# An address change: split operands move from residue 64 and 128 to residue 192 modulo 256 bytes

## What is computed

```python
# first layer
h = rms_norm(x, norm1_w);  proj = h @ w_in                # 2048 x 5648
x = x + concat([attn(q, k, v), ssm(z, xbc, dt)]) @ w_out  # 2048 x 2048
h = rms_norm(x, norm2_w);  u = causal_dwconv(h @ w_up)    # 2048 x 11264
x = x + (silu(u_gate) * u_val) @ w_down                   # 5632 x 2048
# second layer
h = rms_norm_2(x, g) * (1 + scale) + shift
proj = h @ w_in_2                                         # 2048 x 7168
x = x + gate * (concat([y_a, y_r]) @ w_out_2)             # 2048 x 2048
out = rms_norm_2(x, final_gain)
```

## Time and profile before

| what | value |
|---|---|
| median of 3 runs | 1540.4 us (1539.52 to 1541.3) |
| span of the profiled execution | 1537.5 us |
| TensorE busy (matmuls) | 1524.5 us, 12,586 instructions |
| TensorE busy (weight loads) | 1483.7 us |
| VectorE busy | 1136.1 us |
| ScalarE busy | 778.1 us |
| read from memory | 335.97 MB, 220 GB/s over the span |
| granted TensorE clock | full in all 40 slices |

### The profile page before, as it was taken

The page is one execution under the profiler, slowest core; times in us unless marked ns, Lnnn a source line. Parts: engine busy times, 40 slices in busy tenths (PEclk is TensorE's granted clock), DMA queues, the critical chain, the costliest instruction groups (busy, mean ns, idle before and its releaser), DMA issues. The chain is left out here.

```text
span 1537.5 us, 32072 instructions
## 1 busy us (share of the span) xinstructions
PE 1524.5 (99%) x12586; PEld 1483.7 (97%) x12586; DVE 1136.1 (74%) x1373; ACT 778.1 (51%) x930; POOL 29.8 (2%) x56
## 2 busy tenths in 40 slices
PE   9999999999999999999999999999999999999997
PEld 8999997999999999999999999999999989999997
DVE  7877777657987878788788887879854644764754
ACT  7645455545554444444444444445554643454554
POOL 0000000000000000000000000000000000000000
PEclk9999999999999999999999999999999999999999
DMA  9474556457877767677686776866465554445451
GB/s 348 171 272 161 200 177 220 146 171 273 302 282 249 288 233 273 244 249 274 235 293 229 262 272 221 300 219 217 150 247 194 196 193 162 160 159 185 154 186 58
DMA packets 85932, 339.23 MB, mean 221 GB/s; under 512 B 9680, under 2 KB 10208, under 8 KB 79328
## 3 DMA queue, kind: packets, MB, share of 16 engines
q1 hardware_dynamic: 77760, 281.05, 52.1%
q0 software_dynamic: 7232, 54.55, 10.1%
q10 hardware_dynamic: 864, 2.53, 0.4%
HBM read 335.97 MB, written 2.12 MB: 220 GB/s over the span
## 5 line engine op out<-in xcount | busy, mean ns | idle before, releaser
L683 DVE TENSOR_TENSOR wlo<-raw,whi 128x1024 fp32r<-128x1024 f32 x528 | 643.3, 1223 | 345.9 <-ACT whi L320 342.2
L320 ACT ACTIVATE whi<-raw 128x1024 fp32r<-128x1024 f32 x528 | 557.5, 1059 | 646.5 <-PE PS L1328 573.6
L1324 PE MATMUL PS<-gh,whi 128*128 128x256 f32 x3096 | 863.7, 279 | 0.7 <-DVE gl L1208 0.3
L1326 PE MATMUL PS<-gl,whi 128*128 128x256 f32 x3096 | 856.1, 277 | 0.0
L1328 PE MATMUL PS<-gh,wlo 128*128 128x256 f32 x3096 | 856.1, 277 | 0.0
L1324 PEld LDWEIGHTS PS<-gh,whi 128*128 128x128 f32 x3096 | 581.7, 188 | 5.9 <-issue 2.6
L1326 PEld LDWEIGHTS PS<-gl,whi 128*128 128x128 f32 x3096 | 581.4, 188 | 0.8
L1328 PEld LDWEIGHTS PS<-gh,wlo 128*128 128x128 f32 x3096 | 581.6, 188 | 0.0
L1324 PE MATMUL PS<-ah,whi 128*128 128x256 f32 x688 | 189.9, 276 | 0.0
L1328 PE MATMUL PS<-ah,wlo 128*128 128x256 f32 x688 | 189.9, 276 | 0.0
L1326 PE MATMUL PS<-al,whi 128*128 128x256 f32 x688 | 189.9, 276 | 0.0
(11 more groups left out here) (256 smaller groups left out, 894.6 us busy)
## 6 DMA issues: line engine op xcount, KB each, us to landing
raw<-weights SPq DMA_DIRECT2D x528, 512.0 KB, 3.6
ada_w<-w_ada POOLq DMA_DIRECT2D x48, 1024.0 KB, 5.9
EM<-rows POOLq DMA_DIRECT2D x1, 3072.0 KB, 12.4
X<-xT SPq DMA_DIRECT2D x3, 512.0 KB, 8.3
c<-const ACTq DMA_DIRECT2D x1, 1536.0 KB, 7.1
c_act<-c_rows POOLq DMA_DIRECT2D x1, 1024.0 KB, 7.0
outT<-X SPq DMA_DIRECT2D x2, 512.0 KB, 3.2
outT<-X SPq DMA_DIRECT2D x3, 256.0 KB, 2.2
```

The lines of the kernel that those rows point to most:

```text
L320: act.activation(whi[:, j % SPLIT, :], raw[:, j, :], ACT.Copy).then_inc(s_hi, 1)
L683: dve.tensor_tensor(wlo[:, j % SPLIT, :], raw[:, j, :], whi[:, j % SPLIT, :].bitcast(F32), ALU.subtract).then_inc(s_lo, 1)
L1324: pe.matmul(out[:, t, :], whi[:, b, w], hi[:, kt, :], start=first and half == 0 and (apart or t % 2 == 0), stop=False, skip_group_check=True)
L1326: pe.matmul(out[:, t, :], whi[:, b, w], lo[:, kt, :], start=False, stop=False, skip_group_check=True)
```

## The change

It moves addresses; no instruction is added, dropped or moved on any engine.

- The four slots of whi and of wlo are 1,088 numbers long instead of 1,024. 4,352 bytes are 17 times 256, so each slot still begins at residue 128.
- A new function `shifted` gives 16 for the units of the blocks in NAT and NAT2, and 0 for the others. Where it gives 16, ScalarE and VectorE write a unit 16 numbers (64 bytes) further into its slot, and `product_nat` reads it there: its moving operand begins at residue 192 instead of 128.
- The gaps around gh and gl and ahead of ah and ah2 are chosen anew: gh, gl, ah, al, ah2 and al2 begin at residue 192 instead of 64. That is the moving operand of `product` and the stationary one of `product_nat`. The stationary operand of `product` stays at 128.
- Buffers behind gl stand 1,792 bytes further (7 times 256), and SQX2 2,048 bytes; their residues stay.

```diff
--- before.py
+++ after.py
@@ -54,10 +54,18 @@
 
 
 NAT, NAT2 = (9, 10), (6, 7, 10, 13)
+NAT_SHIFT = 16
 CONVERTED = (80, 81, 82, 83, 87, 91)
 OUT_TILES = [8, 9, 10, 11, 12, 13, 14, 15, 0, 1, 2, 3, 4, 5, 6, 7]
 OUT_UNITS = ([(0, k) for k in range(5)] + [(1, k) for k in range(5)] + [(0, 5), (1, 5)] + [(0, 6), (0, 7), (1, 6), (1, 7)]
              + [(2, k) for k in range(8)] + [(3, k) for k in range(8)])
+
+
+def shifted(blk):
+
+    if not isinstance(blk, int):
+        return 0
+    return NAT_SHIFT if blk - B_IN in NAT or blk - B_IN2 in NAT2 else 0
 
 
 def head_tile(low, high, h):
@@ -103,13 +111,12 @@
 
         X, _ = place("X", [P, DT, S])
         raw, _ = place("raw", [P, RAW, 1024])
-        whi, _ = place("whi", [P, SPLIT, 1024], F32R)
-        wlo, _ = place("wlo", [P, SPLIT, 1024], F32R)
-        at[0] += 192
+        whi, _ = place("whi", [P, SPLIT, 1024 + 64], F32R)
+        wlo, _ = place("wlo", [P, SPLIT, 1024 + 64], F32R)
+        at[0] += 64
         gh, _ = place("gh", [P, DT, S], F32R)
-        at[0] += 0
         gl, _ = place("gl", [P, DT, S], F32R)
-        at[0] += 192
+        at[0] += 64
         prm, _ = place("prm", [P, N_PARAMS])
         cst, _ = place("cst", [P, 3 * P + 32])
         rb, _ = place("rb", [P, S])
@@ -150,10 +157,10 @@
         UV, o = place("UV", [P, 4, S + 2], offset=o)
         CG, o = place("CG", [P, 4, S], offset=o)
         CV, o = place("CV", [P, 4, S], offset=o)
-        ah, o = place("ah", [P, 4, S], F32R, offset=o)
+        ah, o = place("ah", [P, 4, S], F32R, offset=o + 128)
         al, o = place("al", [P, 4, S], F32R, offset=o)
-        SQX2, o = place("SQX2", [P, 2, 4, S], offset=o)
-        ah2, o = place("ah2", [P, 4, S], F32R, offset=o)
+        SQX2, o = place("SQX2", [P, 2, 4, S], offset=o + 128)
+        ah2, o = place("ah2", [P, 4, S], F32R, offset=o + 128)
         al2, o = place("al2", [P, 4, S], F32R, offset=o)
 
         TH, _ = place("TH", [P, 8, S], offset=area)
@@ -317,7 +324,8 @@
                 blk, j = blk + j // RAW, j % RAW
                 act.wait_ge(s_raw[j], blk * 16 + 16)
                 act.wait_ge(s_used, blk * RAW + j + 1)
-                act.activation(whi[:, j % SPLIT, :], raw[:, j, :], ACT.Copy).then_inc(s_hi, 1)
+                first = shifted(blk)
+                act.activation(whi[:, j % SPLIT, first:first + 1024], raw[:, j, :], ACT.Copy).then_inc(s_hi, 1)
 
             def group(blk):
                 for j in range(8):
@@ -680,8 +688,9 @@
 
                 blk, j = blk + j // RAW, j % RAW
                 dve.wait_ge(s_hi, blk * RAW + j + 1)
-                dve.tensor_tensor(wlo[:, j % SPLIT, :], raw[:, j, :], whi[:, j % SPLIT, :].bitcast(F32),
-                                  ALU.subtract).then_inc(s_lo, 1)
+                first = shifted(blk)
+                dve.tensor_tensor(wlo[:, j % SPLIT, first:first + 1024], raw[:, j, :],
+                                  whi[:, j % SPLIT, first:first + 1024].bitcast(F32), ALU.subtract).then_inc(s_lo, 1)
 
             def group(blk):
                 for j in range(8):
@@ -1364,7 +1373,7 @@
             def product_nat(b, par, tiles, first, last):
 
                 for half in range(2):
-                    kt, w = tiles[half], slice(512 * half, 512 * half + 512)
+                    kt, w = tiles[half], slice(NAT_SHIFT + 512 * half, NAT_SHIFT + 512 * half + 512)
                     for c in range(2):
                         out, m = PS[:, 2 * par + c, :], slice(P * c, P * c + P)
                         pe.matmul(out, gh[:, kt, m], whi[:, b, w], start=first and half == 0, stop=False,
```

## The result

| | median us | range us | runs |
|---|---|---|---|
| before | 1540.39 | 1539.48 to 1541.3 | 5 |
| after | 1581.84 | 1581.17 to 1582.72 | 5 |

The ratio is 1.027 (95% interval 1.0259 to 1.0281): the kernel is slower, by 41.5 us. The time is inside the range (1514 to 1588), but on the other side than forecast.

What follows compares the result with a forecast made beforehand. The prediction took TensorE's pace through its matmuls to bound the kernel. Its terms, 0 - 3.9 - 1.3 = -5.2 us, took 1540.4 us to 1535 us, with a range of 1514 to 1588.

Steps and rivals of the forecast that it cites:

- What bounds the kernel: Whole kernel: TensorE's pace through its stream of matmuls sets the end; other engines have room for a stream some per cent faster.
- Part 1: ScalarE and VectorE writing 64 bytes further for six blocks, with longer slots: cost 0, either way.
- Part 2: 10,657 fast `product` matmuls, moving residue 64 to 192: pace stays 113.3 ns, cost 0; bounds -15 and +48 us.
- Part 3: 863 `product` matmuls at the slow pace of 117.8 ns fall into the fast pace: -3.9 us.
- The 112 ns of the bare weight load: Loads of 128 stationary columns by themselves, read as 112 ns each; `product` at 113.3 ns stands 1.3 ns above.
- Part 4: 576 `product_nat` matmuls, moving residue 128 to 192, stationary 64 to 192: pitch 228.9 to 226.7 ns, -1.3 us.
- Rival C: `product` stream falls into the slow pace and stays: +48 us for everything, 1588 us; loop alone 1567; chance 0.25.
- Rival E: Distance between the two operands' residues counts: 2.2 ns more on each of 11,520 `product` matmuls, +25 us, 1566 us; chance 0.10.
- Rival B: Pace of `product` itself falls, since 192 is a better start for the moving stream: 1520 us; chance 0.17.
- The rule of the Trainium skill: TensorE has two read ports of its own, one per operand, and never waits; by it the change gives no difference.

## Why the prediction was wrong

- **What bounds the kernel**: right. TensorE's pitch times its matmuls gives the change to 2 us; the other engines only wait longer.
- **Part 1**, the shifted writes and the longer slots cost nothing: right, 1059 and 1224 ns, and the kernel with the activations put back is at 1.0009.
- **Part 2**, the fast pace stays at residue 192: wrong, and this is the step that failed, with part 3: it put a cost of 0 on the move of the moving operand, and 10,356 more matmuls went from 113.3 to 117.8 ns. "0 is nearest to what the trace shows to be reached at one odd multiple of 64 already" looked at the moving operand alone. At the same 192 the loop runs at 113.3 ns with the weights at residue 0 and at 117.8 with them at 128. The upper bound that the part gave, 4.5 x 10,657 = 48 us, is what came, 46 us by the stretches.
- **Part 3**, the 863 slow matmuls become fast (-3.9 us): the opposite, 11,219 are slow. The argument named how the two reads lie to each other as the one thing that differs between the two paces. In the kernel before, the addresses of both paces are the same, so their distance can't be that difference; and the sign was a choice that nothing supported: a new distance could as well favour the slow pace, and it did.
- **The 112 ns of the bare weight load**, which part 2 took as the floor next behind, is not a reading of the earlier trace rows. Those matmuls have a moving stream of 128 columns each, and three of another line just ahead of them (290.86 to 291.18 us) are about 107 ns apart. No run here shows a load by itself.
- **Part 4**, the 512-column form comes to 226.7 ns: right in size (-1 us, -1.3 forecast), by the wrong reason: luck. It isn't the residue 192 that gives it but distance 0: it comes at four residues, and at 192 with the stationary operand at 64 it is 232.4.
- **Rival C** had nearly the right price (1588 forecast, 1581.84 measured) and the wrong cause: chance. In all three kernels at distance +64 the loop and nearly all other stretches are slow. **Rival E** had the right cause, and a price (25 us) carried over from the 512-column form. The runs show that this can't be done: the 512-column form is at its best where the 256-column form is at its worst. With 117.8 ns for the distance +64, which only the runs gave, E would have had C's price.
- **Rival B**, a pace under 113.3 ns: none of the seven distances that ran in the 256-column form went below it, nor did the kernel with the weight reads held still.
- **The rule of the Trainium skill** that the prediction weighed ("SBUF — State Buffer", section "Who interferes with whom"; two read ports of TensorE, which wait on nobody) would have had no difference. The runs differ by 67 us (1540 to 1607) through nothing but addresses, so as the prediction applied it, to the two operands of TensorE itself, it doesn't hold here. The Trainium skill's page "TensorE: Matmul & The Clock Gate", section "Back-to-back issue gap", gives its formula as the gap of an isolated matmul, and says that in a stream of load and matmul pairs both set the spacing; the prediction left this out. The 109.2 ns for 256 columns, an estimate worked out from that formula, was met by no kernel (113.3 at the least).

**Open**: why one distance favours one pace. At -64 some stretches still run at 117.8 (863 matmuls before, 3,371 with the same distance and the weights at 0), and at +64 a few at 113.3 (234): the distance makes one pace likely, it doesn't force it, and what decides the rest isn't known. It isn't drawn anew in each kernel, either: of the 53 to 56 stretches (the loop aside) that can be matched with the kernel before, 45 or 46 have the same pace in each of the three others with gh at 64 and the weights at 128, and only 26 of 54 in the one with 192 and 0. So even at the same distance the two residues themselves, or something that moved with them, have a part outside the loop. A kernel in which the start of the stretches is varied wasn't tried.

## What to carry to other kernels

Where TensorE is bound by matmuls that each have a weight load beside them, measure the pitch for some distances between the two operands' addresses modulo 256 before settling the layout, and measure it for the very form in use: one layout cost 4% here, and the best distance of one form (0 for 512 columns, -64 for 256) was the worst, or among the worst, of the other. An address is judged only together with the other operand's; when one buffer is moved, the other goes with it or the measurement starts anew. And a second pace that some stretches of a trace show without a wait is a warning: a change of layout can spread it over the kernel.

## What the runs showed of the hardware

- In a long stream of matmuls with a weight load beside each, the pitch depends on the distance of the two operands' addresses modulo 256: 113.3 to 120.0 ns for 256 columns of float32r with a load of 128, and 226.7 to 233.3 ns for 512. With the weight load at a fixed address the loop goes from 117.8 to 113.3.
- In the loop the pitch keeps its value to a tenth of a ns over thousands of matmuls: 113.3, 117.8, 118.3, 118.7 or 120.0. Stretches elsewhere, of up to 983 matmuls, have others too at the same distance, 116.7 ns at +32 and 117.3 at -96.
- It changes when the operand does, without a break in the stream: 113.3 ns with gh at 64 and 117.7 with ah at 192 right behind it; 114.8 is the mean of that loop.
